# A hybrid decoder trunk on one core: seven places where the order of the engine programs changes

## The chip, the cores and the metric

The kernel runs on one core of a Trainium2 chip. The metric is the device time of one execution in microseconds (us); less is better. A core has a matrix engine (PE, with its weight loads as PEld), a vector engine (DVE), a scalar engine (ACT), a general engine (POOL, GpSimd) and a queue engine (SP) that here issues the loads. Each engine runs its own program in order; engines wait for one another on semaphores.

## The reference

Two layers. Each normalises x, multiplies it by one large matrix `w_in`, and feeds four token mixers from the product, 256 tokens long: a gated linear recurrence (LRU), a diagonal state space model (S5), retention, and native sparse attention (NSA, with compressed, selected and window keys). Cut to what matters here:

```python
def hybrid_layer(x, ...):
    proj = rms_norm(x, norm_g) @ w_in                 # 1024 -> 10008 columns
    u_lru, u_s5, qkv_ret, q_nsa, kv_nsa, bg_nsa, gate_paths, merge = split_columns(proj, IN_SIZES)
    ys = stack([lru(u_lru), s5(u_s5), retention(qkv_ret), nsa(q_nsa, kv_nsa, bg_nsa)])
    ys = ys * silu(gate_paths)
    branch = einsum('bsnw,nwd->bsnd', ys, w_branch)
    return x + sum(sigmoid(merge) * branch) @ w_out

def nsa(q, kv, bg):                                   # q: 8 heads of 64
    q = rope_half(q, pos, 500000, 16)                 # rotates the first 16 of 64 columns
    k_slc, k_win = rope_half(k_slc, ...), rope_half(k_win, ...)
    s = q @ k * 64 ** -0.5                            # softmax, times v, for each of the three paths
```

S5 needs powers of its complex step (from `exp`, `sin`, `cos` of the layer's parameters), an input matrix, an output matrix and a scan over blocks of four tokens. A final normalisation closes the stack.

## The kernel before, in words

**Tiling.** The large products are cut into chunks (`CHUNKS`, a table with an order written by hand): `u_s5`, `cmp`, `u_lru`, `ret_v`, `nsa_kv`, `ck`, `gate_s5`, `cv`, `gate_lru`, `merge_s5_0`, `merge_s5_1`, `ret_q`, `ret_k`, `nsa_q`, `glu_a`, `glu_b`, `gate_ret` and so on to `out_1b`. A chunk is made of weight units of 512 KB (128 x 1024 float32), numbered from 0; `UNIT_END[CHUNK[name]]` is the number of the unit behind a chunk. u_s5 has units 0 to 3, cmp 4 to 7, u_lru 8 to 11, ret_v 12 to 15, nsa_kv 16 to 19, gate_s5 20 to 23, gate_lru 24 to 27. Chunks write into two PSUM tensors in turn: `pr(name)` is `proj[CHUNK[name] % 2]`, and a chunk starts only when the chunk two before it has been evacuated (`evacuated[0]`, `evacuated[1]`; `evac`, `ev`).

**Three products for one.** Apart from the first three chunks, a unit is loaded by SP into one of four buffers `raw`, copied by ACT in a reduced float32 form as `w_hi` (`cast_units`, one of five slots), and the remainder `w_lo = raw - w_hi` is made by DVE (`split_lo` at L1247, for the chunks of `LO_ON_VECTOR`) or by POOL (`split_lo` at L676). PE multiplies w_hi by h_hi, w_hi by h_lo and w_lo by h_hi. A raw buffer is loaded again when its w_lo is done.

**Order.** Each engine has one program per layer (`@block.sync`, `gpsimd`, `scalar`, `vector`, `tensor`) written out by hand. What ACT does between casts is in small helpers: `next_cast(name)` casts units up to `UNIT_END + 4` and then waits for the chunk, `cast_units(n)` casts all units below n. All ACT operations have the line L698.

**S5 at a layer's start.** DVE makes input weights (`make_w`), ACT spreads them into `wbd` (`spread_w`), PE transposes them (`turn_w`), ACT copies the result (`keep_wT`) and turns the projected input into `uc` by sixteen small copies (`keep_u`). Then `state_inputs`, DVE's `scan_in`, `scan_steps`, `scan_out`, `state_outputs`, ACT's `keep_y`. `make_v` and `spread_v` do the output weights, `chunk_kernels` and `keep_ms` (sixteen copies) the kernel within a block, `angles` and `trig` the phases. All come twice, for half 0 and half 1. `parameters_a` and `parameters_b` work out the powers from the parameters; those of layer 1 run at the end of layer 0.

**The rest.** `compress` multiplies the blocks of keys and values by weights `ck` and `cv` that SP loads by four DMAs of 512 KB (`load_cw1`, at the units in `cw1_at`). `hidden` keeps the result, and a GELU follows (`hid_q`, `hid_tanh`). `rope_nsa` rotates sparse keys (`kd`) and query (`nq4`) in SBUF. `compressed_scores`, a softmax (`cs_sub`, `cs_exp`, `cp_ready`) and the transposes of `cmp_p` are the compressed path.

Of the kernel before, what the change touches and what calls it, by code (L numbers as in the profile page):

```python
# [90 lines left out]
def vector_splits(upto):  # L91
# [19 lines left out]
    "nT_done": 2, "nT_ready": 2, "noT_done": 1, "no_cmp": 1, "nrope_ready": 2, "out_token": 2, "qkT_done": 2,  # L111
    "qkT_ready": 2, "raw_loaded0": 448, "raw_loaded1": 448, "raw_loaded2": 448, "raw_loaded3": 448, "rnT_done": 1,
    "rn_ready": 1, "ro_done": 4, "rope_ready": 2, "rrstd": 1, "rs_done": 4, "rs_ready": 4, "rstd": 2, "rvar": 1,
    "sq": 4, "th_ready": 1, "th_sin": 3, "trig_done": 6, "u_ready": 1, "unit_used": 73, "v0_ready": 1,
    "v_ready": 2, "var": 2, "vbd_ready": 1, "vecT": 2, "vec_ready": 1, "vectors_loaded": 208, "vk_ready": 2,
    "vlo_done": 40, "wT_done": 4, "wT_ready": 4, "w_ready": 2, "wbd_ready": 2, "wl_loaded": 64, "xT_done": 4,
    "x_half": 3, "xc_ready": 1, "y_done": 2, "y_ready": 2, "yg_hi": 4, "yg_lo": 4, "yg_ready": 4, "yr_ready": 1,
    "z_arg": 1, "z_hi": 1, "z_lo": 1, "z_ready": 1, "z_tanh": 1}
# [1964 lines left out]
```

## Time and profile before

| | |
|---|---|
| median of 3 runs | 856.46 us (855.59 to 857.69) |
| the profiled execution | 856.7 us, its span 854.9 us |
| mean granted clock of PE over the span | 0.961 |
| PE busy | 796.3 us, 93% |
| DVE busy | 517.6 us, 61% |
| ACT busy | 450.9 us, 53% |
| POOL busy | 305.2 us, 36% |
| read from HBM | 124.85 MB, 147 GB/s |

The span goes from the first to the last instruction of the profiled execution. A granted clock of 1.00 is 2.4 GHz for PE, 0.50 is 1.2 GHz. Busy shares are means over stages of very different kinds: PE is busy for most of the span, and the other engines feed it. Layer 0 covers roughly the first 433 us, layer 1 the rest, with the same order of work.

### The profile page before, as it was taken

To read this page: it belongs to the slowest core of one execution; us is meant where nothing else is said; L and a number is where in the kernel's file an instruction comes from. 1 tells how busy PE (TensorE), PEld (TensorE's weight loads), DVE (VectorE), ACT (ScalarE), POOL (GpSimd) and SP (SyncE) were. 2 spreads that over 40 slices of the span, in tenths; PEclk is the share of its full clock that TensorE was granted. 3 is DMA by queue.
4 is the path that set the end of the run, shared out by engine and by line. 5 is a ranking of instruction groups with operands and counts; after the bars stand their busy time and mean duration, and the time that the engine had idled before them with its cause. 6 is when DMAs were issued, how large, how long until landed. Compare 5 with 4: busy or idle time off the path is not lost.

```text
span 854.9 us, 11525 instructions
## 1 busy us (share of the span) xinstructions
PE 796.3 (93%) x4446; PEld 680.7 (80%) x4446; DVE 517.6 (61%) x761; ACT 450.9 (53%) x781; POOL 305.2 (36%) x135
## 2 busy tenths in 40 slices
PE   8786999899989899999989979998998989999996
PEld 8675889688978688887878868986897868888885
DVE  2957394477698551534686575547868875435335
ACT  5555786345752356553447297654474534545542
POOL 3000000005468576657400000000256775655860
PEclk9977999999998799999999989999999998999999
DMA  8518355466245434345435663535635344345541
GB/s 250 140 50 289 99 176 178 138 191 193 88 117 169 134 118 153 102 150 171 145 78 140 196 216 94 204 123 165 211 121 156 114 137 127 126 129 170 173 148 49
DMA packets 86998, 126.64 MB, mean 148 GB/s; under 512 B 22072, under 2 KB 32672, under 8 KB 86944
## 3 DMA queue, kind: packets, MB, share of 16 engines
q1 hardware_dynamic: 86768, 125.88, 47.5%
q8 instruction: 35, 0.57, 0.3%
q14 instruction: 19, 0.16, 0.1%
q10 hardware_dynamic: 176, 0.04, 0.0%
HBM read 124.85 MB, written 1.05 MB: 147 GB/s over the span
## 4 chain that ended last, share of the span: by engine, by line
PE 73%; ACT 9%; DVE 8%; issue 5%; POOL 2%; DMA 2%; ACTq 0%; POOLq 0%; DVEq 0%
PE proj L1662 52%; PE proj L1701 5%; PE M L1657 3%; ACT sc L698 2%; DMA raw<-in_w_in 2%; POOL w_lo L676 2%; PE M L1823 2%; ACT nkT L698 1%; ACT qT L698 1%; PE M L1976 1%; PE M L1981 1%; DVE sc L1539 1%; PE M L559 1%; ACT w_hi L698 1%; PE M L1824 1%
## 5 line engine op out<-in xcount | busy, mean ns | idle before, releaser
L676 POOL TENSOR_TENSOR w_lo<-raw,w_hi 128x1024 fp32r<-128x1024 f32 x112 | 287.1, 2596 | 501.2 <-ACT w_hi L698 469.9
L698 ACT ACTIVATE w_hi<-raw 128x1024 fp32r<-128x1024 f32 x192 | 197.4, 1055 | 125.0 <-DMA raw<-in_w_in 68.1
L1662 PE MATMUL proj<-w_hi,h_hi 128*128 128x512 f32 x544 | 220.5, 405 | 8.2 <-DVE w_lo L1247 7.7
L1662 PE MATMUL proj<-w_lo,h_hi 128*128 128x512 f32 x544 | 215.6, 396 | 0.0
L1662 PE MATMUL proj<-w_hi,h_lo 128*128 128x512 f32 x544 | 215.2, 396 | 0.0
L1662 PEld LDWEIGHTS proj<-w_hi,h_hi 128*128 128x128 f32 x544 | 104.3, 192 | 31.7 <-DVE w_lo L1247 8.5
L1662 PEld LDWEIGHTS proj<-w_hi,h_lo 128*128 128x128 f32 x544 | 104.2, 192 | 22.8
L1662 PEld LDWEIGHTS proj<-w_lo,h_hi 128*128 128x128 f32 x544 | 104.4, 192 | 21.0 <-issue 0.5
L1247 DVE TENSOR_TENSOR w_lo<-raw,w_hi 128x1024 fp32r<-128x1024 f32 x80 | 94.8, 1221 | 38.5 <-ACT w_hi L698 27.1
L1701 PE MATMUL proj<-h_full,raw 128*128 128x256 f32 x256 | 59.3, 393 | 7.8 <-ACT u_s L698 7.8
L1701 PEld LDWEIGHTS proj<-h_full,raw 128*128 128x128 f32 x256 | 50.1, 198 | 15.5 <-ACT u_s L698 8.3
L698 ACT ACTIVATE sc<-sc,st 128x256 f32<-128x256 f32 x64 | 28.3, 448 | 57.2 <-DVE st L1555 57.2
L1662 PE MATMUL proj<-w_hi,ys_hi 128*128 128x512 f32 x128 | 52.7, 412 | 0.6 <-POOL w_lo L676 0.5
L1662 PE MATMUL proj<-w_lo,ys_hi 128*128 128x512 f32 x128 | 51.7, 404 | 0.0
L1662 PE MATMUL proj<-w_hi,ys_lo 128*128 128x512 f32 x128 | 51.4, 402 | 0.0
L698 ACT ACTIVATE qT<-M 32x128 f32<-32x128 f32 (+1 forms) x68 | 29.5, 433 | 35.2 <-PE M L1657 25.9
L1662 PE MATMUL proj<-h_hi,w_hi 128*128 128x256 f32 x128 | 36.9, 288 | 3.1 <-ACT nv L698 3.1
L1290 DVE SCALAR_TENSOR_TENSOR mt<-mt,proj 128x1024 f32<-128x1024 f32 x12 | 14.7, 1221 | 38.5 <-PE proj L1662 38.5
L1662 PE MATMUL proj<-h_lo,w_hi 128*128 128x256 f32 x128 | 36.2, 283 | 0.0
L1662 PE MATMUL proj<-h_hi,w_lo 128*128 128x256 f32 x128 | 36.2, 283 | 0.0
L1662 PEld LDWEIGHTS proj<-w_hi,ys_hi 128*128 128x128 f32 x128 | 25.2, 197 | 7.3 <-issue 1.3
L1662 PEld LDWEIGHTS proj<-w_hi,ys_lo 128*128 128x128 f32 x128 | 25.1, 196 | 5.5
(330 smaller groups left out, 1294.0 us busy)
## 6 DMA issues: line engine op xcount, KB each, us to landing
raw<-in_w_in SPq DMA_DIRECT2D x152, 512.0 KB, 3.7
raw<-in_w_branch SPq DMA_DIRECT2D x32, 512.0 KB, 3.6
raw<-in_w_out SPq DMA_DIRECT2D x16, 512.0 KB, 3.6
raw<-in_s_w_glu SPq DMA_DIRECT2D x8, 512.0 KB, 4.5
raw<-in_w_in SPq DMA_DIRECT2D x8, 256.0 KB, 2.6
merged<-in_nsa_ck_w SPq DMA_DIRECT2D x4, 512.0 KB, 5.2
mt<-in_nsa_ck_w SPq DMA_DIRECT2D x4, 512.0 KB, 6.8
merged<-in_nsa_cv_w SPq DMA_DIRECT2D x4, 512.0 KB, 4.6
```

What stands on the lines that cost most here:

```text
L559: last = nc.tensor.matmul(M[:, k // 2, at:at + P], x[:, t, k * P:(k + 1) * P], diag[:, t, :], start=True, stop=True)
L676: nc.gpsimd.tensor_tensor(w_lo[:, slot(s, l), 0:n * w], raw[:, u % N_RAW, 0:n * w], w_hi[:, slot(s, l), 0:n * w].bitcast(f32), ALU.subtrac ...
L698: i = nc.scalar.activation(out_, in_, func, **kw)
L1247: v.tensor_tensor(w_lo[:, slot(s, l), 0:w], raw[:, u % N_RAW, 0:w], w_hi[:, slot(s, l), 0:w].bitcast(f32), ALU.subtract).then_inc(vlo_done, 1)
L1290: v.scalar_tensor_tensor(m, m, 1.0, src, ALU.add, ALU.mult).then_inc(evac(full), 1)
L1539: i = v.tensor_tensor(cp[:, e_], cmp_s[:, e_], bc(coef[:, e_].unsqueeze(3), shape), ALU.mult)
L1657: return nc.tensor.transpose(dst, src, ident[0:rows_, 0:rows_])
L1662: last = mm(dst, left[i], right[j], start=start and n == 0, stop=stop and n == 2, skip_group_check=True)
L1701: last = mm(ps[:, m * T:(m + 1) * T], rw[:, m * P:(m + 1) * P], h_full[:, k, :], start=st_ and m % 2 == 0, stop=sp_, skip_group_check=True)
L1823: mm(dst, vk[:, f, s, 1:LC + 1].rearrange("p k g c -> p (k g c)"), s5_h[:, f, s, :], start=f == 0, stop=False)
L1824: last = mm(dst, ms[:, s, :], uc[:, HS * h + s, :], start=False, stop=True)
L1976: last_ = mm(M[:, 2, at:at + P], nqT[r, 2 * h + n, 0:P], nkT[r, i, 0:P], start=True, stop=True)
```

## The change

- `u_s5` is evacuated on ACT right behind its chunk, ahead of `spread_w(0)`; `keep_v0` goes ahead of `trig(0)`; `keep_u` reads the SBUF copy.
- `spread_v(0)` goes behind the copies of `cmp`; `u_lru` is evacuated behind three casts fewer; `spread_w(1)` goes ahead of the casts of units 15 and 16, `keep_ms(0)` behind them; the four `ck` loads go from ahead of unit 15 to ahead of unit 17.
- The copies of `nsa_kv` no longer stand behind two casts.
- `hid_tanh` goes ahead of `merge_chunk("s5", 0)`.
- The exponential of the compressed scores goes ahead of the `qT` copy.
- The rotation of the keys moves to behind `skip(1)`; that of the query to behind `rope_ret(1, "ret_k")`, reading PSUM, with the factor 64 ** -0.5 in new constants; `chunk("glu_b")` on PE waits for its reads.
- The second part of `parameters_b` becomes `parameters_c` and runs at the start of the next layer's DVE program.

The table of semaphore counts and the removed helper are left out of the diff.

```diff
@@ sync
-                    cw1_at = {UNIT_END[CHUNK["u_lru"]] + 3: "ck", UNIT_END[CHUNK["gate_s5"]] + 2: "cv"}
+                    cw1_at = {UNIT_END[CHUNK["ret_v"]] + 1: "ck", UNIT_END[CHUNK["gate_s5"]] + 2: "cv"}
@@ scalar
-                        src = pr("u_s5")[:, :].rearrange("p (q c j) -> p q c j", q=KB, j=LC)[:, :, :, LC - 1 - e]
+                        src = u_s5[:, :, :].rearrange("p q (c j) -> p q c j", j=LC)[:, :, :, LC - 1 - e]
...
+                    next_cast("u_s5")
+                    run(flat(u_s5[:, :, :]), pr("u_s5")[:, :], ACT.Copy, evac("u_s5"))
                     spread_w(0)
+                    keep_v0()
                     trig(0)
-                    keep_v0()
-                    next_cast("u_s5")
+                    act.wait_ge(evac("u_s5"), ev("u_s5"))
                     keep_u(0)
                     keep_u(1)
                     keep_wT(0, 0)
                     keep_u(2)
                     keep_u(3)
-                    run(flat(u_s5[:, :, :]), pr("u_s5")[:, :], ACT.Copy, evac("u_s5"))
                     keep_wT(0, 1)
-                    spread_v(0)
...
                     run(bgate[:, :, :], cm[:, :, 256:CMP_W], ACT.Tanh, cmp_read, scale=0.5)
+                    spread_v(0)
...
-                    next_cast("u_lru")
+                    cast_units(UNIT_END[CHUNK["u_lru"]] + 2)
+                    act.wait_ge(chunk_done, ch("u_lru"))
                     run(u_lru[:, :, 3:T + 3], pr("u_lru")[:, :].rearrange("p (t n) -> p t n", t=KB), ACT.Copy, evac("u_lru"))
+                    cast_units(UNIT_END[CHUNK["u_lru"]] + 3)
+                    spread_w(1)
+                    cast_units(UNIT_END[CHUNK["ret_v"]])
+                    keep_wT(1, 0)
                     cast_units(UNIT_END[CHUNK["ret_v"]] + 1)
-                    spread_w(1)
                     keep_ms(0)
-                    keep_wT(1, 0)
                     next_cast("ret_v")
...
-                    next_cast("nsa_kv")
+                    act.wait_ge(chunk_done, ch("nsa_kv"))
...
-                    merge_chunk("s5", 0)
                     act.wait_ge(hid_arg, 1)
                     run(hid_q, hid_q, ACT.Tanh, hid_tanh, scale=GELU_C)
+                    merge_chunk("s5", 0)
...
+                    act.wait_ge(cs_sub, 1)
+                    run(cols(3072, 256), cols(3072, 256), ACT.Exp, cs_exp)
                     act.wait_ge(rnT_done, 1)
                     run(flat(qT[:, :, :]), MF[:, 1024:2048], ACT.Copy, yr_ready)
-                    act.wait_ge(cs_sub, 1)
-                    run(cols(3072, 256), cols(3072, 256), ACT.Exp, cs_exp)
@@ vector
                         link(v.tensor_tensor(S(17), S(19), S(16), ALU.subtract))
+
+                    def parameters_c(s):
+
+                        stage = Layer(vector, s)
                         stage.wait_ge(th_sin, 3)
...
+                    parameters_c(l)
                     v.memset(u_lru[:, :, 0:3], 0.0)
...
+                    nk4 = kd[:, :, :, :, :, :].rearrange("p a y h u d -> p a (y h u) d")
+
+                    def rotate(src, dst, at, read):
+
+                        shape = [P, TT, NHQ, 8]
+                        cos, sin = (bc(cst(f"nsa_{f}{at}").rearrange("p (a c) -> p a c", a=TT).unsqueeze(2), shape) for f in ("cos", "sin"))
+                        x1, x2_ = src[:, :, :, 0:8], src[:, :, :, 8:16]
+                        v.tensor_tensor(rope_n[:, 0], x1, cos, ALU.mult)
+                        v.tensor_tensor(rope_n[:, 1], x2_, sin, ALU.mult)
+                        v.tensor_tensor(rope_n[:, 2], x2_, cos, ALU.mult)
+                        v.tensor_tensor(rope_n[:, 3], x1, sin, ALU.mult).then_inc(read, 1)
+                        dve.wait_ge(read, 1)
+                        v.tensor_tensor(dst[:, :, :, 0:8], rope_n[:, 0], rope_n[:, 1], ALU.subtract)
+                        v.tensor_tensor(dst[:, :, :, 8:16], rope_n[:, 2], rope_n[:, 3], ALU.add).then_inc(nrope_ready, 1)
...
                     skip(1)
+                    rotate(nk4, nk4, "", nk_read)
                     split_lo("merge_s5_0", 0)
...
-                    dve.wait_ge(evac("nsa_kv"), ev("nsa_kv"))
-                    dve.wait_ge(rope_ready, 2)
-                    rope_nsa(rope_nsa_kd)
-
+                    dve.wait_ge(evac("nsa_q"), ev("nsa_q"))
                     dve.wait_ge(nrope_ready, 1)
+                    rotate(pr("nsa_q")[:, :].rearrange("p (a h c) -> p a h c", a=TT, h=NHQ), nq4, "_q", nq_read)
+
+                    dve.wait_ge(nrope_ready, 2)
...
-                    dve.wait_ge(evac("nsa_q"), ev("nsa_q"))
-                    dve.wait_ge(yg_ready, 1)
-                    rope_nsa(nq4)
                     gate_times("ret")
@@ tensor
+                    pe.wait_ge(nq_read, 1)
                     chunk("glu_b")
```

## Rows read from the trace of the kernel before

**Rows 1.** Waits of PE: who waited for whom, us in total, times, longest.
```profile
PE M L1657 <- ACT gate L698: 13.0, 2, 7.1
PE M L1657 <- DVE sc L1539: 8.5, 2, 4.2
PE proj L1701 <- ACT u_s L698: 7.8, 2, 7.2
PE proj L1662 <- DVE w_lo L1247: 7.7, 2, 3.8
PE M L559 <- DVE diag L552: 4.6, 2, 3.7
PE M L1657 <- DVE u_s L1433: 4.1, 2, 2.0
PE proj L1662 <- ACT nv L698: 3.1, 2, 1.6
```

**Rows 2.** Windows: length, busy PE, PEld, DVE, ACT, POOL, granted clock, DMA share.
```profile
45.70:51.50 5.80, 5.76 (x14) 4.54 (x15) 4.04 (x19) 4.39 (x9) 0.00 (x0) 0.50 0.01 3
80.30:85.60 5.30, 5.25 (x17) 4.48 (x18) 5.20 (x8) 5.08 (x17) 0.00 (x0) 0.50 0.66 169
163.50:167.50 4.00, 4.00 (x11) 3.13 (x12) 3.30 (x3) 0.59 (x1) 0.00 (x0) 0.58 0.65 212
273.40:280.20 6.80, 6.80 (x21) 5.50 (x21) 1.33 (x4) 0.00 (x0) 1.99 (x1) 0.50 0.47 153
290.60:297.20 6.60, 6.57 (x23) 5.44 (x24) 1.93 (x3) 1.33 (x2) 4.51 (x2) 0.50 0.73 213
...
497.80:502.00 4.20, 4.20 (x14) 3.72 (x15) 4.17 (x5) 4.04 (x15) 0.00 (x0) 0.50 0.69 165
...
662.50:665.90 3.40, 3.40 (x10) 2.63 (x9) 2.11 (x5) 3.35 (x4) 0.00 (x0) 0.50 0.22 85
705.40:713.70 8.30, 8.30 (x27) 6.79 (x28) 3.63 (x4) 1.37 (x3) 4.43 (x2) 0.50 0.69 210
```

**Rows 3.** Timeline of ACT in layer 0: start us, us, what, [idle before].
```profile
28.31 0.42 ACT L698 ACTIVATE gate<-qT 64x256 f32<-64x256 f32 x1 [7.66 <-DVE sc L1154]
...
41.55 3.08 ACT L698 ACTIVATE nkT<-proj 32x256 f32<-32x256 f32 x8
...
110.62 2.01 ACT L698 ACTIVATE w_hi<-raw 128x1024 fp32r<-128x1024 f32 x2
...
114.26 4.92 ACT L698 ACTIVATE s5x<-M 32x64 f32<-32x64 f32 x16
```

**Rows 4.** Chain of waits in layer 1: start us, us, what.
```profile
485.16 7.13 DMA raw<-in_w_in
...
506.39 0.87 PE M L1657 x8
507.26 5.47 PE proj L1662 x24
```

**Rows 5.** Timeline of DVE in layer 0.
```profile
68.14 1.23 DVE L1247 TENSOR_TENSOR w_lo<-raw,w_hi 128x1024 fp32r<-128x1024 f32 x1 [1.12 <-ACT w_hi L698]
...
71.74 1.20 DVE L1205 TENSOR_TENSOR_SCAN sc<-sc 128x512 f32<-128x512 f32 x1
...
77.16 0.68 DVE L1217 TENSOR_TENSOR s5x<-sc 128x504 f32<-128x504 f32 x1
...
87.40 3.50 DVE L1247 TENSOR_TENSOR w_lo<-raw,w_hi 128x1024 fp32r<-128x1024 f32 x3 [0.23 <-ACT w_hi L698]
```

**Rows 6.** Timeline of DVE at hid's tanh, layer 0.
```profile
158.19 0.23 DVE L1375 TENSOR_SCALAR kT<-kT 128x128 f32<-128x128 f32 x1 [8.93 <-ACT kT L698]
```

**Rows 7.** Timeline of DVE behind the exponential, layer 0.
```profile
282.33 0.50 DVE L1529 TENSOR_TENSOR sc<-sc,const 128x128 f32<-128x128 f32 x2 [6.49 <-ACT sc L698]
```

**Rows 8.** DVE's groups, 200 to 246 us: busy us, mean ns, idle before.
```profile
L1428 DVE TENSOR_TENSOR sc<-u_s,const 128x128 f32<-128x128 f32 x1 | 2.5, 2475 | 0.0
```

**Rows 9.** Timeline of DVE at the layers' border.
```profile
435.81 0.68 DVE L1635 SCALAR_TENSOR_TENSOR x<-proj,x 128x512 f32<-128x512 f32 x1
```

More of the change, by code:

```diff
@@ L110 @@
     "mT_done": 2, "mag_arg": 1, "mag_exp": 1, "mhi_done": 2, "mlo_done": 2, "ms_ready": 2, "mt_free": 6,
[L111 to L118, printed above, removed]
+    "nT_done": 2, "nT_ready": 2, "nk_read": 1, "noT_done": 1, "no_cmp": 1, "nq_read": 1, "nrope_ready": 2,
+    "out_token": 2, "qkT_done": 2, "qkT_ready": 2, "raw_loaded0": 448, "raw_loaded1": 448, "raw_loaded2": 448,
+    "raw_loaded3": 448, "rnT_done": 1, "rn_ready": 1, "ro_done": 4, "rope_ready": 2, "rrstd": 1, "rs_done": 4,
+    "rs_ready": 4, "rstd": 2, "rvar": 1, "sq": 4, "th_ready": 1, "th_sin": 3, "trig_done": 6, "u_ready": 1,
+    "unit_used": 73, "v0_ready": 1, "v_ready": 2, "var": 2, "vbd_ready": 1, "vecT": 2, "vec_ready": 1,
+    "vectors_loaded": 208, "vk_ready": 2, "vlo_done": 40, "wT_done": 4, "wT_ready": 4, "w_ready": 2,
+    "wbd_ready": 2, "wl_loaded": 64, "xT_done": 4, "x_half": 3, "xc_ready": 1, "y_done": 2, "y_ready": 2,
+    "yg_hi": 4, "yg_lo": 4, "yg_ready": 4, "yr_ready": 1, "z_arg": 1, "z_hi": 1, "z_lo": 1, "z_ready": 1,
+    "z_tanh": 1}
 TWO_PI = 2.0 * math.pi
@@ L131 @@
 for _n, _s in (("ident", P), ("ret_cos", TT * 64), ("ret_sin", TT * 64), ("nsa_cos", TT * 8), ("nsa_sin", TT * 8),
+               ("nsa_cos_q", TT * 8), ("nsa_sin_q", TT * 8),
                ("cmp_cos", 8), ("cmp_sin", 8), ("decay", NH_RET * T), ("causal", 2 * P), ("cmp_add", TT * 16),
@@ L160, in shape_constants @@
     put("nsa_cos", c), put("nsa_sin", s)
+    put("nsa_cos_q", c * f32(HD ** -0.5)), put("nsa_sin_q", s * f32(HD ** -0.5))
     c, s = rope((np.arange(32) % 16) * 16 + 31, 500000.0, HD // 4)
@@ L360, in hybrid_trunk @@
             "at_even", "at_s", "at_max", "at_exp", "at_pT", "at_pT_ready", "at_o", "at_no"))
-        noT_done = sem("noT_done")
+        noT_done, nk_read, nq_read = sem("noT_done"), sem("nk_read"), sem("nq_read")
         mT_done, mhi_done, mlo_done = sem("mT_done"), sem("mhi_done"), sem("mlo_done")
@@ L1420, in _ @@
                     rope_ret(1, "ret_k")
-                    def rope_nsa(x4):
-                        shape = [P, TT, NHQ, 8]
-                        cos = bc(cst("nsa_cos").rearrange("p (a c) -> p a c", a=TT).unsqueeze(2), shape)
-                        sin = bc(cst("nsa_sin").rearrange("p (a c) -> p a c", a=TT).unsqueeze(2), shape)
-                        x1, x2_ = x4[:, :, :, 0:8], x4[:, :, :, 8:16]
-                        v.tensor_tensor(rope_n[:, 0], x1, cos, ALU.mult)
-                        v.tensor_tensor(rope_n[:, 1], x2_, sin, ALU.mult)
-                        v.tensor_tensor(rope_n[:, 2], x2_, cos, ALU.mult)
-                        link(v.tensor_tensor(rope_n[:, 3], x1, sin, ALU.mult))
-                        v.tensor_tensor(x1, rope_n[:, 0], rope_n[:, 1], ALU.subtract)
-                        v.tensor_tensor(x2_, rope_n[:, 2], rope_n[:, 3], ALU.add).then_inc(nrope_ready, 1)
-                    rope_nsa_kd = kd[:, :, :, :, :, :].rearrange("p a y h u d -> p a (y h u) d")
-                    dve.wait_ge(evac("nsa_kv"), ev("nsa_kv"))
-                    dve.wait_ge(rope_ready, 2)
-                    rope_nsa(rope_nsa_kd)
+                    dve.wait_ge(evac("nsa_q"), ev("nsa_q"))
                     dve.wait_ge(nrope_ready, 1)
+                    rotate(pr("nsa_q")[:, :].rearrange("p (a h c) -> p a h c", a=TT, h=NHQ), nq4, "_q", nq_read)
+                    dve.wait_ge(nrope_ready, 2)
                     dve.wait_ge(chunk_done, ch("glu_a"))
```

## The prediction

> **What bounds the kernel now.** I read the waits of PE first, then the granted clock by stretch, then the timelines of ACT and DVE around each wait. PE stands still for 51.7 us of the 854.9 us span (the sum of its idle stretches); for the rest it works, so only what ends a PE wait, or what makes a matmul quicker, can move the end. [rows 1] shows that nearly all of it has a few releasers, each met once a layer: ACT's spread of the S5 weights (13.0), DVE's product for the compressed attention (8.5), ACT's copy of the S5 input (7.8), a DVE remainder w_lo (7.7), the diagonal at a layer's end (4.6, of which 3.7 at the border of the layers), the rotated sparse query (4.1) and ACT's copy of the sparse keys and values (3.1). The second view is the windows of [rows 2]: after most of these waits the granted clock is 0.50, the 1.2 GHz level, for 3.4 to 8.3 us in which PE works. There are ten such stretches; the four short ones are shown by their first and last. Their PE busy times are 5.8, 5.3, 6.8, 6.6, 4.2, 8.3 and four of about 3.4, together 50.5 us. At half clock half of that is lost: 25.3 us. The waits and the low clock together are 77 us, the most that an order of the queues could give.
>
> **Seven edits, part by part.** The sum is made against the profiled execution: span 854.9 us, time 856.7 us (0.24 above the median of 856.46).
>
> 1. *u_s5 evacuated first.* proj[0] comes free for u_lru only when ACT has copied u_s5; before, that copy stood behind sixteen small copies (keep_u), two wT copies, trig(0) and spread_w(0). Now it follows the chunk at once, and keep_u reads the copy in SBUF. In layer 0 PE's 7.2 goes, in layer 1 its 0.7: the 7.8 of [rows 1]. What is late next: state_inputs(0), which wants keep_u and both wT copies. In layer 1 ACT now blocks on the chunk before it does spread_w(0) and trig(0). After the chunk it has 15.8 us of work (copy 1.0, spread_w 2.5, keep_v0 1.6, trig 2.6, twice 3.1 of keep_u, twice 1.0 of wT), while PE has some 17.2 (turn_c, cmp, two turn_w, half of u_lru). 1.3 us of cover, so the cost is nothing; without cover each us is a us.
> The keep_u copies change their source. In [rows 3] eight 256-column copies from PSUM took 3.08, 0.385 each, and one from SBUF 0.42: sixteen cost 0.6 more, and 0.7 of cover stays. The Trainium skill (VectorE: DVE Perf Modes, "The TRN2 errata") speaks against this edit here: it has ScalarE pay 52 cycles more per instruction from SBUF than from PSUM. By its figure sixteen copies are 0.7 us more, an estimate; the trace agrees, and the sum would be the same by either.
>
> 2. *ck loads two units later, spread_w(1) ahead of the fourth cast.* Before, turn_w(1, 0) waited 7.1 and 6.0: ACT sat on the cast of unit 15 before spread_w(1), and that unit landed 7.1 us after its issue [rows 4] because four 512 KB loads of the compression weights stood ahead of it on SP. Now SP sends units 15 and 16 first and spread_w(1) needs only chunk_kernels(0). The 13.0 of [rows 1] goes. The ck weights come some 3 us later and are wanted only at compress, more than 25 us on, so that move costs nothing; SP's wait on v_ready and vk_ready holds unit 17 only, by then both are there.
> What is late next is DVE. Let T be the end of chunk_kernels(0). ACT has unit 14's w_hi at T+1.0 (u_lru is done at T-1.1, copy, cast). From the start of that w_lo, DVE takes 4.8 to the end of scan_steps (68.14 to 72.94), then w_lo 15 1.2, then 10.0 from the first line of scan_out to the end of angles(1) (77.16 to 87.17), then w_lo 17 1.2 [rows 5]: unit 17 is ready at T+18.2. PE wants it after two half chunks of 5.7, two transposes of 1.0 and a unit of 2.75 ([rows 4], 5.5 and 0.9 without overlap): T+16.2. A **new wait of about 2.1 us** in each layer, 4.2. Bounds: 0 if DVE's small gaps close, 4 each if keep_ms(0), which now stands ahead of cast 17, meets a late load.
>
> 3. *Two casts taken from ahead of the kv copies.* nv is ready 2.0 sooner, so the 3.1 of [rows 1] goes. But casts 22 and 23 now follow keep_ms(1). With N the end of nsa_kv: kv copies to N+1.9, keep_ms 4.9, casts 2.0 [rows 3], the hidden copy 0.4: N+9.2; PE has kernels 1.1, compress 1.9 and six us of gate_s5 and wants it at N+8.8. w_lo 22 is at N+9.0, scan_out 3.8 behind it, w_lo 23 at N+13.9, wanted at N+12.6. **New waits of 0.4 and 1.3**, less overlap 1.6 a layer, 3.2 in all: this edit gives nothing. Bounds 2 and 5.
>
> 4. *hid's tanh ahead of merge_chunk(s5, 0).* DVE stood 8.9 for it [rows 6] and then still had three operations of the GELU before the w_lo that PE waited for. ACT passes that place some ten us sooner, DVE has the argument by then, so the cast units behind it wait for nothing. DVE has ten us of slack: the 7.7 goes.
>
> 5. *Exponential ahead of the qT copy.* DVE stood 6.5 for it [rows 7], and its next three operations on two SBUF inputs each lasted as long as a POOL w_lo. Its argument is ready at 275.8, the copy ahead of it at 282.0. The 8.5 goes, with some five us to spare; next late is yr_ready, over before PE gets there. For that the qT copy is 0.4 later at most.
>
> 6. *Sparse rotations.* The key rotation moves to a DVE gap of 2.0 after skip(1), where POOL has no w_lo; six operations at the 0.25 of [rows 7] are 1.5, covered. The query rotation reads PSUM straight after ret_k's. In its old place each of four operations lasted 2.5 [rows 8]. The 4.1 of [rows 1] goes and DVE has 15 us less in a layer. Added: glu_b waits for nq_read. DVE gets the copy at 208.1, four operations, read by 209.5, wanted at 216.9: covered by lru_mm and glu_a. The last two have both inputs in SBUF and may last 2.5 each; glu_a's evacuation, queued behind them, is due at 216.4, so still nothing.
>
> 7. *parameters_c behind the layer's border.* The last half of x was added at 435.81 [rows 9], though PE had been done since 433.3 (its 3.7 wait before 437.0). 2.5 goes, 1.2 stays. Its 4.3 us now lie ahead of layer 1's S5 preparation: w_ready at about 445.6, wanted by ACT only after the u_s5 chunk, at 453.
>
> **Sum.** Waits: 7.8 + 13.0 + 3.1 + 7.7 + 8.5 + 4.1 = 44.2, plus 2.5 = 46.7, less 4.2 and 3.2: 39.3. Clock: 25.3 now. In two places the trace is split: the 273.4 stretch has no long idle ahead of it, only the compressed scores' tiny matmuls, and layer 1 had none there; and a 2.05 wait was followed by a low stretch in layer 1 (662.5) but not in layer 0. So I keep 3.4 for the first and 1.7 for one of the two new 2.1 waits, 5.1 in all; 20.2 comes back. 39.3 + 20.2 = 59.5, and 856.7 - 59.5 = 797.2; I say **797**.
>
> **Rivals.**
> - *The feeding side takes over in the first third* (17 in 100): ACT's and DVE's queues are fuller than my two chains show, and the waits at units 17 and 23 grow to 4 and 2.5 each with low clock behind them. Against my 7.4: 13.0, and some 5 of clock; 807, and 812 with half of edit 4 lost. For it: DVE is busy in almost all of that stretch. Against it: both layers have the same queues and the chain adds up from rows.
> - *The clock does not come back* (10 in 100): the low stretches belong to the kind of work, not to the waits. All 20.2 stay: 817. For it the 273.4 stretch; against it, eight of the ten stand right behind a wait.
> - *No new wait* (8 in 100): my two chains are too long by a few us each and the clock is full. 797.2 - 7.4 - 5.1 = 784.7.
> - *An edit does not bite* (3 in 100): one copy or load is released by something else than the trace names, of the size of edit 2: 13.0 + 4.7 of clock, 814.
> - *Slower* (2 in 100): one mechanism, PE's clock over dense stretches. With the waits gone PE works almost without rest, and if a dense stretch itself brought 1.2 GHz, each 10 us of it would cost 5. The gain is gone from about 120 us of it on top, over the kernel; now there are 50.5, none of them in a dense stretch. From there it is slower, 860 for 126 us.
>
> **How the numbers follow.** Forecast 60 in 100, its own range 790 to 804. With 784.7 on one side and 807 to 817 on the other, 784 to 816 leaves out under 2 in 10. The measurement tells 0.3% (2.6 us) from nothing; only the last rival and a mishap I don't see lie there: faster 0.95, same 0.02, slower 0.03.
>
> **What would show it.** After: no PE wait on u_s or gate of over 1 us; on w_lo of DVE four waits of 1 to 2.5, at unit 17 of nsa_kv and unit 23 of gate_s5; mean clock from 0.961 to about 0.99; DVE's rotations about 0.3 each and POOL's w_lo a little shorter. Wrong if state_inputs(0) of layer 1 waits for u_ready (edit 1's cover was too small), if cast 17 waits on a DMA, or if low-clock stretches stand where no wait is.

## The result, and the profile after

The changed kernel takes **816.65 us** (median of 4 runs, 812.21 to 819.84), the kernel before 856.03 on the same chip: a ratio of 0.9537, 95% interval 0.9475 to 0.9598. That is 39.4 us less, where 59.5 were forecast, and the time lies 0.65 above the forecast's range. The profiled execution took 819.8 us. From the page of the changed kernel, its span, the busy time of PE and PE's granted clock in 40 slices:

```profile
span 818.0 us, 11525 instructions
PE 788.7 (96%) x4446; PEld 677.6 (83%) x4446; DVE 479.4 (59%) x761; ACT 459.3 (56%) x781; POOL 304.3 (37%) x135
...
PEclk9979899999999999999999899999999989999999
```

Two subtractions divide the result. Span less PE busy went from 58.6 to 29.3: 29.3 us less standing still, against 39.3 forecast. PE busy went from 796.3 to 788.7: 7.6 us back from the clock, against 20.2. So of the profiled run's 22.6 us above the forecast, 10.0 are waits and 12.6 are matmuls that ran at the lower level. ACT, with the same 781 instructions, is 8.4 us busier than the 450.9 of before; that is the trace of the cause, as the copies below show.

The waits of PE after, where [rows 1] had those of before (waiter, releaser, us in total, times, longest; L1673 is the old L1662, L1807 is `state_inputs`, L701 is ACT's one line):

```profile
PE M L1807 <- ACT s5x L701: 7.6, 2, 4.2
PE proj L1673 <- DVE w_lo L1259: 7.6, 4, 2.6
PE proj L1673 <- POOL w_lo L679: 2.0, 4, 0.8
PE M L562 <- DVE diag L555: 1.9, 2, 1.1
PE proj L1750 <- ACT kT L701: 1.5, 2, 0.8
```

Every wait that the edits aimed at is gone: gate, the product `sc`, `u_s` of ACT and of DVE, `nv`. The first line is new and was forecast as nothing: `state_inputs(0)` waits once a layer for `keep_wT`. The second has nearly the sum that it had in [rows 1] (7.7) by chance: it is now unit 17 (2.63 and 2.60) and unit 23 (1.20 twice), which were forecast at 2.1 and 1.3.

The chain that ended last shows the first line's making. Layer 1, from the end of the u_s5 chunk (start us, us, what):

```profile
424.96 6.92 PE proj L1712 x32
...
432.83 1.23 ACT gate L701 x3
434.06 0.01 issue
434.07 1.23 ACT gate L701 x3
...
438.08 1.34 ACT sc L701 x3
439.42 0.57 ACT nkT L701
439.99 0.01 issue
440.00 0.68 ACT nkT L701
...
451.24 1.03 ACT s5x L701
452.27 0.14 issue
452.41 5.42 PE M L1807 x32
```

The chain leaves PE at 431.88 and comes back to it at 452.41. In between ACT hardly rests: copy of u_s5, `spread_w(0)`, `keep_v0`, `trig(0)`, sixteen `keep_u` (nkT) and two `keep_wT`. That is 20.4 us to 452.27; PE had work until 448.95. The length of the sixteen, from the timeline of ACT (start us, us, what):

```profile
439.32 5.48 ACT L701 ACTIVATE nkT<-u_s 32x256 f32<-32x256 f32 x8
444.81 1.02 ACT L701 ACTIVATE s5x<-M 128x1024 f32<-128x1024 f32 x1
445.86 5.36 ACT L701 ACTIVATE nkT<-u_s 32x256 f32<-32x256 f32 x8
```

Eight copies take 5.48 and 5.36, 0.67 to 0.68 each, where [rows 3] has eight from PSUM in 3.08. Same shape, same type, same count; only the source is another.

The windows of low clock, where [rows 2] had ten (length, busy PE, PEld, DVE, ACT, POOL, granted clock, DMA share, GB/s). There are six, besides one at the very end:

```profile
10.50:13.90 3.40, 3.40 (x17) 3.40 (x17) 0.25 (x4) 0.00 (x0) 0.00 (x0) 0.50 1.00 396
51.50:61.70 10.20, 10.20 (x41) 9.48 (x41) 2.99 (x6) 6.36 (x12) 0.00 (x0) 0.50 0.00 0
85.60:92.40 6.80, 6.20 (x17) 5.03 (x18) 4.04 (x4) 5.80 (x9) 0.00 (x0) 0.50 0.71 231
263.10:266.50 3.40, 3.40 (x9) 2.66 (x10) 2.75 (x9) 0.42 (x1) 1.40 (x1) 0.50 0.48 164
454.20:461.00 6.80, 6.80 (x28) 6.30 (x28) 1.85 (x4) 4.86 (x10) 0.00 (x0) 0.50 0.02 4
659.00:665.80 6.80, 6.80 (x22) 5.70 (x22) 3.60 (x13) 0.42 (x1) 2.46 (x1) 0.50 0.54 157
```

PE works 36.8 us in them at 0.50, the 1.2 GHz level, and loses half, 18.4. The second and the fifth begin 0.6 and 1.8 us behind the new wait (PE works again from 50.86 and 452.41) and cost 8.5 of the 18.4. The first stands at the first transposes of layer 0; the profile of before has none there, and four of the twelve kernels below have one, so no single edit brings it. The third stands at unit 17's wait of layer 0, and layer 1, with the same wait, has none. The fourth and the sixth stand at the compressed scores with no wait ahead of them.

Four more answers to rows of before, in the timeline of DVE: the first GELU operation behind hid's tanh [rows 6], the product behind the exponential [rows 7], the last of the six operations of the query's rotation [rows 8], and the last half of x at the border [rows 9].

```profile
146.54 0.22 DVE L1403 TENSOR_SCALAR kT<-kT 128x128 f32<-128x128 f32 x1
...
265.26 0.49 DVE L1540 TENSOR_TENSOR sc<-sc,const 128x128 f32<-128x128 f32 x2 [0.48 <-ACT sc L701]
...
200.70 2.47 DVE L1319 TENSOR_TENSOR u_s<-sc 128x128 f32<-128x128 f32 x1
...
413.21 0.69 DVE L1646 SCALAR_TENSOR_TENSOR x<-proj,x 128x512 f32<-128x512 f32 x1 [0.94 <-PE proj L1673]
```

In the edited places DVE's waits on ACT of 8.93 and 6.49 are gone or 0.48, and x is added right behind PE.

### The profile page after: what moved, and what is told of

Read it like the earlier page. It is cut to its first block, busy times and chain, and to the rows that moved or that the text cites. A ratio compares the mean times of both kernels' runs of the same rounds, so it can differ in the third digit from the quotient of the medians.

```text
span 818.0 us, 11525 instructions
## 1 busy us (share of the span) xinstructions
PE 788.7 (96%) x4446; PEld 677.6 (83%) x4446; DVE 479.4 (59%) x761; ACT 459.3 (56%) x781; POOL 304.3 (37%) x135
## 4 chain that ended last, share of the span: by engine, by line
PE 72%; issue 9%; DVE 8%; ACT 7%; POOL 4%; DMA 1%; POOLq 0%; DVEq 0%; SPq 0%; ACTq 0%
PE proj L1673 52%; POOL w_lo L679 4%; PE proj L1712 3%; ACT nkT L701 3%; PE M L1668 2%; PE M L1807 2%; DVE w_lo L1259 2%; PE M L1834 2%; ACT sc L701 1%; PE M L1988 1%; PE M L562 1%; PE M L1993 1%; PE M L1958 1%; PE M L1835 1%; PE M L2012 1%
## 5 line engine op out<-in xcount | busy, mean ns | idle before, releaser
L701 ACT ACTIVATE w_hi<-raw 128x1024 fp32r<-128x1024 f32 x192 | 197.2, 1053 | 95.9 <-PE proj L1673 60.0
L1673 PE MATMUL proj<-w_hi,h_hi 128*128 128x512 f32 x544 | 219.3, 403 | 6.7 <-DVE w_lo L1259 5.2
L1673 PE MATMUL proj<-w_lo,h_hi 128*128 128x512 f32 x544 | 214.7, 395 | 0.0
L1673 PE MATMUL proj<-w_hi,h_lo 128*128 128x512 f32 x544 | 214.5, 394 | 0.0
L1673 PEld LDWEIGHTS proj<-w_hi,h_hi 128*128 128x128 f32 x544 | 103.6, 190 | 30.1 <-DVE w_lo L1259 6.1
L1673 PEld LDWEIGHTS proj<-w_hi,h_lo 128*128 128x128 f32 x544 | 103.7, 191 | 22.4
L1673 PEld LDWEIGHTS proj<-w_lo,h_hi 128*128 128x128 f32 x544 | 103.8, 191 | 20.7 <-issue 0.5
L701 ACT ACTIVATE sc<-sc,st 128x256 f32<-128x256 f32 x64 | 28.2, 442 | 49.4 <-DVE st L1566 49.4
L1673 PE MATMUL proj<-w_hi,ys_hi 128*128 128x512 f32 x128 | 50.9, 397 | 0.5 <-POOL w_lo L679 0.5
L1673 PE MATMUL proj<-w_lo,ys_hi 128*128 128x512 f32 x128 | 49.9, 390 | 0.0
L1673 PE MATMUL proj<-w_hi,ys_lo 128*128 128x512 f32 x128 | 49.9, 390 | 0.0
L701 ACT ACTIVATE qT<-M 32x128 f32<-32x128 f32 (+1 forms) x68 | 29.5, 434 | 19.1 <-PE M L1668 12.5
L1673 PE MATMUL proj<-h_hi,w_hi 128*128 128x256 f32 x128 | 37.1, 290 | 2.4 <-DVE w_lo L1259 2.4
L1673 PE MATMUL proj<-h_lo,w_hi 128*128 128x256 f32 x128 | 36.2, 283 | 0.0
L1673 PE MATMUL proj<-h_hi,w_lo 128*128 128x256 f32 x128 | 36.2, 283 | 0.0
L701 ACT ACTIVATE s5x<-M 32x64 f32<-32x64 f32 (+4 forms) x72 | 27.0, 375 | 5.0 <-PE M L1668 4.2
L1673 PEld LDWEIGHTS proj<-w_hi,ys_hi 128*128 128x128 f32 x128 | 24.0, 188 | 6.0 <-issue 0.8
```

The source lines that it names most:

```text
L701: i = nc.scalar.activation(out_, in_, func, **kw)
L1673: last = mm(dst, left[i], right[j], start=start and n == 0, stop=stop and n == 2, skip_group_check=True)
```

## Experiments

Theory A: the reads of `keep_u` are the fault. It takes every fourth value of u_s5 (`(c j)` with a fixed j), which from PSUM cost 0.385 and from SBUF 0.68; the new wait and the clock behind it follow. Rival B: the chain on ACT is too long anyhow with the chunk in its middle. Rival C: the clock stays low for reasons other than waits. The recorded expectations letter their own theories anew, run by run. Then each edit was undone alone, to see which term of the sum is of the wrong size.

| kernel | median us | span, profiled | PE busy | span less PE busy |
|---|---|---|---|---|
| before | 856.03 | 854.9 | 796.3 | 58.6 |
| changed | 816.65 | 818.0 | 788.7 | 29.3 |
| adjacent reads | 799.09 | 800.7 | 778.7 | 22.0 |
| trig(0) later | 802.35 | 799.6 | 773.8 | 25.8 |
| both of these | 798.63 | 796.7 | 774.5 | 22.2 |
| edit 1 undone | 805.68 | 803.0 | 772.1 | 30.9 |
| edit 2 undone | 832.37 | 831.9 | 791.8 | 40.1 |
| edit 3 undone | 817.31 | 815.8 | 786.7 | 29.1 |
| edit 4 undone | 829.27 | 827.4 | 790.2 | 37.2 |
| edit 5 undone | 827.58 | 824.4 | 786.1 | 38.3 |
| edit 6 undone | 821.3 | 819.1 | 785.3 | 33.8 |
| edit 7 undone | 817.22 | 822.0 | 790.2 | 31.8 |
| scores in two halves | 800.1 | 798.6 | 775.8 | 22.8 |
| three repairs | 794.13 | 791.5 | 775.3 | 16.2 |

Each median is of 4 runs. The kernel before was timed again beside each group of runs, with medians of 855.57 to 856.76; the changed kernel was timed once, so every difference below shares its 816.65 and its scatter. A time that goes up and down from run to run does so with the clock: the changed kernel's four were 819.78, 813.52, 812.21 and 819.84 us at mean granted clocks of 0.976, 0.984, 0.986 and 0.976. One per cent of clock is some 8 us, so the last two columns, from one execution each, must be read beside the median. The waits repeat from profile to profile (the 7.6 on DVE's w_lo stands in seven of these kernels); the clock does not.

### Adjacent reads for keep_u

```diff
-  src = u_s5[:, :, :].rearrange("p q (c j) -> p q c j", j=LC)[:, :, :, LC - 1 - e]
+  src = u_s5[:, :, :].rearrange("p q (j c) -> p q j c", j=LC)[:, :, LC - 1 - e, :]
...
-  run(flat(u_s5[:, :, :]), pr("u_s5")[:, :], ACT.Copy, evac("u_s5"))
+  run(u_s5[:, :, :].rearrange("p q (j c) -> p q j c", j=LC),
+      pr("u_s5")[:, :].rearrange("p (q c j) -> p q j c", q=KB, j=LC), ACT.Copy, evac("u_s5"))
```

The copy of the chunk turns the order, so that `keep_u` reads runs of 64 adjacent values; DVE's one reader of u_s5 follows.

> The changed kernel with one edit: the copy of u_s5 is written with each token's place in its block outermost, so that keep_u reads 64 contiguous values per row instead of every fourth; skip reads u_s5 through the same view. Theory A (the stride): from SBUF every fourth value is what made keep_u 0.68 us each instead of 0.385; contiguous they go to 0.42, ACT is 4.2 us earlier a layer, the waits of 4.2 and 3.4 at state_inputs(0) go to under 0.6 and the low-clock stretch behind each (10.2 and 6.8 us) goes with them: 816.7 - 7.0 - 8.5 = about 801. Theory B (the source, not the stride): any copy of 256 columns from SBUF to 32 partitions costs 0.68, the waits and the time stay within 2 us of 816.7.

Measured: 799.09 us (797.51 to 802.48), ratio 0.9334 (0.9302 to 0.9367). The timeline of ACT in layer 1 and the last line of the waits of PE:

```profile
428.99 3.39 ACT L701 ACTIVATE nkT<-u_s 32x256 f32<-32x256 f32 x8
...
PE M L1809 <- ACT s5x L701: 0.2, 1, 0.2
```

Eight copies in 3.39, 0.42 each: the very figure that the prediction took from one small copy in [rows 3]. The wait of 7.6 is 0.2, and the time is 2 us from the forecast 797.2. In the profiled runs 7.3 us of standing still and 10.0 of PE busy have gone. A holds, and the theory of the recorded text that any copy from SBUF costs 0.68 whatever its stride falls. B falls too: the order of ACT's queue is the same and the wait is gone. C falls for most of the loss: PE busy is 17.6 under that of before, though the work is the same; four low stretches are left. Here is the same stretch of PE's timeline in layer 1, of the changed kernel and then of this one:

```profile
452.41 5.42 PE L1807 MATMUL M<-nkT,s5x 128*128 128x64 f32 x32 [3.46 <-ACT s5x L701]
```

```profile
438.45 3.68 PE L1809 MATMUL M<-nkT,s5x 128*128 128x64 f32 x32
```

The wait has gone, and the products behind it are 1.7 us quicker.

### trig(0) behind the weights

The reads stay every fourth value; only 2.5 us of other work leave the chain, `trig(0)` going behind `keep_wT(0, 1)`.

```diff
                     keep_v0()
-                    trig(0)
...
                     keep_wT(0, 1)
+                    trig(0)
```

> The changed kernel with trig(0) moved behind keep_wT(0, 1) on ACT; keep_u still reads every fourth value from SBUF. Theory A (ACT's queue between the u_s5 copy and keep_wT(0, 1) sets state_inputs(0)): the waits fall by trig's 2.6 us, from 4.2 and 3.4 to 1.6 and 0.8, and the low clock behind them shrinks or goes: 816.7 - 5.2 - 0 to 8 = 803 to 811. Theory B (something else releases state_inputs, such as u_lru's loads): same time, the waits stay.

Measured: 802.35 us (801.4 to 810.4), ratio 0.9398 (0.9341 to 0.9455). Waits of PE:

```profile
PE proj L1673 <- DVE w_lo L1259: 8.6, 4, 3.1
PE M L1807 <- ACT s5x L701: 2.2, 2, 1.1
```

Shortening the chain by 2.5 took 5.4 of the 7.6 away, and unit 17's waits grew by 0.5 each. So the wait is one of the chain's length, as A and B both have it, and its price is far more than its length: 14.3 us of median for 4.4 us of waits. The rest is clock: two stretches of 3.4 us in this profile instead of six with 37.4. The time lies just under the 803 to 811 expected.

### Both repairs

> Two repairs of edit 1 at once: the copies of kept u read adjacent values, and trig(0) stands behind the weights of the keep. Either alone takes the wait ahead of state_inputs(0) away or to about 1 us (799.09 and 802.35). If that wait is the whole cost of edit 1's miss, the two together give what adjacent reads alone give, 798 to 800. If the length of the copies on ScalarE costs something elsewhere too, or trig(0) does where it stands, the two differ: below 796 would show the second, above 802 the lateness of trig(0) at unit 17.

Measured: 798.63 us (798.52 to 798.74), ratio 0.9329 (0.9315 to 0.9343). Not to be told from adjacent reads alone, as expected if the wait is the whole cost of edit 1's miss. Once ACT is within PE's 17.1 us, more room there is worth nothing that these runs show.

### Each edit undone

*Edit 1*: `keep_u` reads PSUM again (that line is left out here) and u_s5 is evacuated behind it.

```diff
-                    next_cast("u_s5")
-                    run(flat(u_s5[:, :, :]), pr("u_s5")[:, :], ACT.Copy, evac("u_s5"))
                     spread_w(0)
-                    keep_v0()
                     trig(0)
+                    keep_v0()
+                    next_cast("u_s5")
...
                     keep_u(3)
+                    run(flat(u_s5[:, :, :]), pr("u_s5")[:, :], ACT.Copy, evac("u_s5"))
```

> The changed kernel with edit 1 undone: u_s5 copied last, keep_u from PSUM, trig and spread_w as before. By my ledger edit 1 took out a wait of 7.2 and 0.7 and put in 4.2 and 3.4, so it is worth about nothing in waits: the time is 817 give or take 3, with a wait of 7 us on u_s in layer 0 and under 1 in layer 1. By the prediction's step it was worth 7.8 us plus 2.9 of clock: 827.

Measured: 805.68 us (804.64 to 813.1), ratio 0.9424 (0.9376 to 0.9473): faster with the edit undone, by 11.0 in the medians, though one of its four runs (813.1) lies above the changed kernel's lowest (812.21). Neither number expected. In PE's timeline of layer 0 and the one window of low clock of this kernel:

```profile
45.92 8.82 PE L1711 MATMUL proj<-h_full,raw 128*128 128x256 f32 x32 [7.13 <-ACT u_s L701]
...
42.50:49.30 6.80, 3.38 (x8) 2.75 (x9) 6.49 (x19) 6.69 (x16) 0.00 (x0) 0.50 0.01 2
```

The waits are as long as with the edit (30.9 against 29.3 of standing still): the edit exchanged 7.8 of old waits and 0.6 of a small one for 7.6 of new ones. The difference is PE busy, 772.1 against 788.7, 16.6 less in two profiled executions that lie 15.0 apart. Against the kernel with adjacent reads, undoing the edit costs 6.6 us (805.68 to 799.09): with the right reads edit 1 does pay, for the 7.8 of waits that it removes. Half of the low window here falls into the wait itself, where it costs nothing; in the changed kernel PE worked through all 17.0 us of the two behind `state_inputs`. Its four other stretches (two of them at the compressed scores) aren't in this profile either, and no row says why. One of the four runs, at 813.1 and a clock of 0.982 instead of 0.994, had some, by its clock.

*Edit 2*: `ck` loads, casts, `spread_w(1)`, `spread_v(0)` and the u_lru copy as before.

```diff
-  cw1_at = {UNIT_END[CHUNK["ret_v"]] + 1: "ck", ...
+  cw1_at = {UNIT_END[CHUNK["u_lru"]] + 3: "ck", ...
...
-                    cast_units(UNIT_END[CHUNK["u_lru"]] + 3)
-                    spread_w(1)
-                    cast_units(UNIT_END[CHUNK["ret_v"]])
-                    keep_wT(1, 0)
                     cast_units(UNIT_END[CHUNK["ret_v"]] + 1)
+                    spread_w(1)
                     keep_ms(0)
+                    keep_wT(1, 0)
```

> The changed kernel with edit 2 undone: ck loads ahead of unit 15, spread_w(1) behind the cast of unit 15, spread_v(0) and the u_lru copy in their old places. By the prediction's ledger: the waits of 7.1 and 6.0 at turn_w(1, 0) come back with 4.7 of clock, and the two of 2.6 at unit 17 of nsa_kv go: 816.7 + 13.1 - 5.2 + 1 to 5 = 826 to 830. Rival, that with edit 1 in its slow form ACT's delay at state_inputs(0) is passed on and the load is early enough: under 820.

Measured: 832.37 us (825.8 to 833.7), ratio 0.9714 (0.9673 to 0.9754): the edit is worth 15.7. Waits of PE:

```profile
PE M L1665 <- ACT gate L701: 15.0, 2, 8.4
...
PE proj L1670 <- DVE w_lo L1256: 2.4, 2, 1.2
```

15.0 come back and unit 17's 5.2 go, 9.8 net (13.0 less 4.2 forecast, 8.8). The time is above the 826 to 830 expected. In the profiled pair, 13.9 apart, standing still is 10.8 and PE busy 3.1 longer; this profile has seven low stretches with some 54 us, in part inside waits, instead of six with 37.4.

*Edit 3*: the two casts ahead of the nsa_kv copies again.

```diff
-                    act.wait_ge(chunk_done, ch("nsa_kv"))
+                    next_cast("nsa_kv")
```

> The changed kernel with edit 3 undone: casts 22 and 23 ahead of the nsa_kv copies. The prediction had it worth nothing: waits of 1.6 a layer on nv come back, and those at hidden_T and unit 23 of gate_s5 (0.8 and 1.2) go: within 1.5 us of 816.7. Rival, that it was worth its full 3.1: 820.

Measured: 817.31 us (816.7 to 819.41), ratio 0.9546 (0.9518 to 0.9573). Waits of PE:

```profile
PE proj L1673 <- DVE w_lo L1259: 5.2, 2, 2.6
PE proj L1673 <- ACT nv L701: 3.1, 2, 1.6
```

3.1 back on nv; the kT line (1.5) and unit 23 (2.4) gone. It is the exchange that the prediction worked out, and the time doesn't move.

*Edits 4 and 5*: `merge_chunk("s5", 0)` ahead of hid's tanh again, and the `qT` copy ahead of the exponential again.

The recorded expectation of edit 4 names two exponential and copy steps, which are edit 5's; the edit that was run, and the 7.7 us that it is about, are edit 4's.

```diff
+                    merge_chunk("s5", 0)
                     run(hid_q, hid_q, ACT.Tanh, hid_tanh, scale=GELU_C)
-                    merge_chunk("s5", 0)
```

> Edit 4 alone is undone: order of the two exponential and copy steps as before. Prediction's step: it removed 7.7 us of waits. If it holds, these waits come back and nothing else moves: 816.65 + 7.7 = 824, and up to 828 if a stretch of low clock (3.4 us each, as the changed kernel's rows have them) follows each of the waits. Rival: what was gained there is taken back by the next wait, so undoing it costs under 3 us, 817 to 820.

```diff
-                    act.wait_ge(cs_sub, 1)
-                    run(cols(3072, 256), cols(3072, 256), ACT.Exp, cs_exp)
                     act.wait_ge(rnT_done, 1)
                     run(flat(qT[:, :, :]), MF[:, 1024:2048], ACT.Copy, yr_ready)
+                    act.wait_ge(cs_sub, 1)
+                    run(cols(3072, 256), cols(3072, 256), ACT.Exp, cs_exp)
```

> The changed kernel with edit 5 undone: the exponential behind the qT copy. By the ledger a wait on DVE's L1539 line of up to 4.2 a layer comes back with 3 to 4 of low clock each; but DVE's three operations there may now meet another state of POOL. 816.7 + 8.5 + 7.5 = 833 if all of it; rival, that POOL's contention was a matter of timing and the wait is shorter now: 820 to 826.

Measured: 829.27 us (828.83 to 829.36), ratio 0.9686 (0.967 to 0.9702), and 827.58 (823.78 to 829.01), ratio 0.9666 (0.9638 to 0.9694). Edit 4 is worth 12.6 (829.27 is above the 824 to 828 expected), edit 5 10.9 (827.58 lies between the 833 of the full price and the rival's 820 to 826). From the waits and the windows of the first, then of the second:

```profile
PE proj L1673 <- DVE w_lo L1259: 15.3, 6, 3.8
...
156.50:163.20 6.70, 5.08 (x12) 4.02 (x13) 4.97 (x5) 1.49 (x2) 0.00 (x0) 0.50 0.55 182
559.30:566.00 6.70, 5.90 (x14) 4.65 (x15) 4.55 (x5) 2.29 (x3) 0.00 (x0) 0.50 0.68 208
```

```profile
PE M L1668 <- DVE sc L1550: 8.4, 2, 4.2
...
272.20:279.00 6.80, 5.37 (x20) 4.53 (x21) 2.14 (x2) 1.33 (x2) 5.91 (x3) 0.50 0.78 229
675.00:681.70 6.70, 5.72 (x21) 4.79 (x22) 2.04 (x2) 1.33 (x2) 5.45 (x3) 0.50 0.79 233
```

The waits come back at their old length (15.3 less 7.6 is 7.7; 8.4), all four with a low stretch that reaches on behind them, some 11 us of work at half speed in either kernel, 5.5 lost. 7.7 + 5.5 is 13.2 for 12.6 measured; 8.4 + 5.5 is 13.9 for 10.9. That sum is not shown as the cause of the medians: PE busy of the whole profile is only 1.5 above the changed kernel's with edit 4 undone and 2.6 below it with edit 5 undone, because other stretches were shorter or missing (behind the wait at `state_inputs` of layer 0, 6.8 us instead of 10.2 with edit 5 undone).

*Edit 6*: both rotations in their old places, in SBUF.

```diff
-                    rotate(nk4, nk4, "", nk_read)
...
-                    rotate(pr("nsa_q")[:, :].rearrange(...), nq4, "_q", nq_read)
+                    rotate(nk4, nk4, "", nk_read)
...
+                    rotate(nq4, nq4, "", nq_read)
...
-                    pe.wait_ge(nq_read, 1)
```

> Edit 6 alone is undone. Prediction's step: 4.1 us of waits. If it holds, 816.65 + 4.1 = 821, up to 824 with one stretch of low clock more per layer (1.7 us each). Rival: hidden by what is late next, 816 to 818.

*Edit 7*: `parameters_c` of layer 1 at the end of layer 0 again.

```diff
-                    parameters_c(l)
+                    if l == 0:
+                        parameters_c(0)
...
+                        parameters_c(l + 1)
```

> Edit 7 alone is undone. Prediction's step: 2.5 us of waits. If it holds, 816.65 + 2.5 = 819, up to 822 with a stretch of low clock. Rival: hidden by what is late next, 816 to 818.

Measured: 821.3 us (820.92 to 824.13), ratio 0.9601 (0.9583 to 0.9619), and 817.22 (816.1 to 823.82), ratio 0.9562 (0.9523 to 0.9602). The line that came back in each, from the waits of PE:

```profile
PE M L1670 <- DVE u_s L1319: 4.1, 2, 2.0
```

```profile
PE M L562 <- DVE diag L555: 4.5, 2, 3.7
```

4.1 and 2.6 of waits, as forecast. Edit 6 is worth 4.7 by the medians; all four of its runs lie above all four of the changed kernel's, the nearest two by 1.1. For edit 7 the medians show 0.6, which the runs (816.1 to 823.82) can't tell from the 2.5 of its wait nor from nothing.

The seven together: -11.0 + 15.7 + 0.7 + 12.6 + 10.9 + 4.7 + 0.6 = 34.2, against 39.4. The 5.2 between are no more than the scatter by the clock, and the seven differences share one median: were it 1 us off, the sum would be 7 off.

### The compressed scores in two halves

On top of adjacent reads, the second half of the 32 tiny products is moved one call on, to see whether they are what lowers the clock there.

```diff
                     compressed_scores(0)
-                    compressed_scores(1)
...
+                    compressed_scores(1)
```

> The kernel contig (799.1) with the second half of the compressed scores moved behind the next weight unit on PE, so that its 32 tiny products come as 16 and 16. Theory A (the low clock of 3.4 and 6.8 us there belongs to the stretch of tiny products): it goes, 1.7 + 3.4 less, 794 to 796, and runs scatter less. Theory B (it follows from something else): the stretches stay, 799 give or take 1.5.

Measured: 800.1 us (799.25 to 800.44), ratio 0.935 (0.9336 to 0.9364). The windows around both places and the low ones of this profile:

```profile
76.70:80.10 3.40, 3.40 (x9) 2.63 (x8) 1.22 (x2) 3.37 (x7) 0.00 (x0) 0.50 0.88 267
250.00:257.00 7.00, 7.00 (x43) 5.94 (x43) 2.16 (x7) 0.82 (x2) 2.71 (x1) 1.00 0.45 157
465.80:472.60 6.80, 6.16 (x17) 5.05 (x18) 4.08 (x4) 5.03 (x8) 0.00 (x0) 0.50 0.71 221
640.00:649.00 9.00, 9.00 (x59) 7.91 (x60) 4.20 (x7) 0.86 (x2) 4.71 (x2) 1.00 0.49 175
```

The clock stays at the 2.4 GHz level at the scores now, but one profile in which it does is no proof (those of edit 1 undone and of trig(0) later have no stretch there either, with the products together). The stretch at unit 17 came in layer 1 as well, 6.8 us where adjacent reads alone had none, and the time is that of adjacent reads alone: the stretches go as theory A has it, the time is theory B's. Whether the tiny products lower the clock stays open.

### Three repairs in one kernel

Adjacent reads, and the two new waits that the prediction had named: unit 17's w_lo ahead of DVE's `angles(1)`, and casts 22 and 23 ahead of `keep_ms(1)` but still behind the nsa_kv copies.

```diff
+                    cast_units(UNIT_END[CHUNK["nsa_kv"]] + 4)
...
+                    split_lo("nsa_kv", 1)
...
-                    split_lo("nsa_kv", 1, 2, 3)
+                    split_lo("nsa_kv", 2, 3)
```

> The kernel contig (799.1) with two more moves: split_lo of unit 17 of nsa_kv ahead of angles(1) on DVE, and casts 22 and 23 ahead of keep_ms(1) on ACT. If the waits of 2.6 at unit 17 (twice) stand behind angles(1) alone and those of 1.2 at unit 23 (twice) behind keep_ms(1), both go down to 0.3 or less: 799.1 - 4.8 - 2.2 = 792, and 790 with the low clock behind the first. Rival, that ACT's keep_ms(0), still ahead of cast 17, or a late load holds unit 17: 796 to 799.

Measured: **794.13 us** (788.5 to 795.9), ratio 0.927 (0.9227 to 0.9313), the fastest here. Waits of PE:

```profile
PE proj L1754 <- ACT kT L701: 2.4, 2, 1.2
PE proj L1677 <- POOL w_lo L679: 2.0, 4, 0.7
...
PE proj L1677 <- ACT nv L701: 1.0, 2, 0.5
```

No wait on DVE's w_lo is left: 7.6 go, 0.9 come on kT and 1.0 on nv. Standing still falls from 22.0 to 16.2, 5.8, for 5.0 of median. Because of the 1.9 that came back elsewhere, the time lies between the 790 to 792 expected and the rival's 796 to 799. All lines of its waits together are 9.2 us, the most that ending waits could still give; the clock is on top, three stretches of 3.4 us in this profile, and the run of 788.5 had a mean granted clock of 0.998 where the profiled one, 793.37, had 0.992.

## Why the prediction was wrong, step by step

**Edit 1 failed: its "so the cost is nothing".** `state_inputs(0)` was to wait for nothing and waited 7.6 us. Two things were wrong in that step. First the price of the source. The prediction took 0.42 for a copy from SBUF, from a row whose source lies in runs of adjacent values, and put it to a copy that takes every fourth float; that was 0.68. It made sixteen copies cost 0.6 us more where they cost 4.7 (10.84 against 6.16). The rest of that chain was right: 15.8 and 4.7 make 20.5, where 20.4 were measured, and PE's cover was 17.1 for 17.2. So 1.3 of cover became waits of 3.4 in layer 1 and 4.2 in layer 0, the case that the last lines of the prediction name as the one to make it wrong. Second, layer 0's chain wasn't added up at all; there DVE's phases hold ACT up for 0.8 more. The row for the right price was missing from the trace of before, and then both ends should have stood: 0.42 and something well above it. At 0.68 the step would have said 3.4 us of wait a layer, and with 1.7 to 4.2 of clock behind each (the stretches of 3.4 to 8.3 us in [rows 2]) 807 to 812. The measured median is 4 above that still: the rest is the clock, below.

The Trainium skill has the rule (Advanced Engine Details and Errata, "SBUF Cachelines"): SBUF is read in lines of 16 bytes, and a reader that goes to another line with each access pays for it. Every fourth float32 lies 16 bytes from the last, and the trace agrees with the direction: 0.68 us against 0.42 for 256 values. The prediction weighed another place of the Trainium skill (VectorE: DVE Perf Modes, "The TRN2 errata"), by which ScalarE pays 52 cycles more per instruction from SBUF than from PSUM. Adjacent reads bear it out (3.39 for eight against 3.08); the reads as written cost far more.

**The clock term was mis-sized.** Forecast 20.2 back of 25.3; the changed kernel's profile gives 7.6 of busy time. That profile is near the changed kernel's slow end, 3.1 above its median. 10.0 of the 12.6 missing came back with adjacent reads, so they hung on the wait at `state_inputs` or went with it. The remainder is what the prediction treated too firmly: which waits have a stretch behind them. Unit 17's wait of 2.6 had one in layer 0 of the changed kernel (6.8) and none in layer 1; with the scores in two halves it was longer in layer 1; the compressed scores, which it took as one stretch of 3.4, had 3.4 and 6.8. From run to run the changed kernel moves by 7.6 us in this way. The 5.1 kept for what stays should have been a range: the four kernels with the new wait repaired and the wait at unit 17 left kept some 3 to 8.4 (half of the work in the low stretches). Why a wait has a stretch behind it in one layer or run and not in another, no run here shows.

**What held.** Unit 17: 2.1 forecast, 2.6 measured; unit 23: 1.3 and 1.2; hidden's copy 0.4 and 0.8; the border 1.2 left and 1.1. Edits 4, 5, 6 and 7 took away the waits that they were said to, to 0.1 us by the lines that undoing them brings back; edit 2's came back at 15.0 for 13.0. The medians move the same way for edits 2, 4, 5 and 6: 15.7, 12.6, 10.9 and 4.7. Edit 3 gave nothing, as worked out. With adjacent reads both terms of the sum come out close: the forecast makes 19.3 of standing still and 776.1 of PE busy, the profile has 22.0 and 778.7, in the slowest of its four runs. Two of the rotation's operations were allowed 2.5 each; one took it (2.47), the other five 0.3, and none mattered. Not foreseen: PE waits 2.0 on POOL's w_lo, 1.0 before.

**The rivals.** The measured time is that of "the clock does not come back" (817), but that is chance: its reason, that the work itself holds the clock down, does not hold. With the same kind of work, five kernels above had PE busy of 772 to 776. (The prediction counts eight of the ten low stretches of before behind a wait; by the trace it is nine, all but that of 273.4.) "The feeding side takes over" named units 17 and 23 with 4 and 2.5; they had 2.6 and 1.2. What happened was in no rival: the feeding side, at another place.

## What to carry to other kernels

When a change gives an instruction another source, its price is that of the new memory at the same stride, so look for a row with both, and where there is none, keep both ends. Add up the whole queue between a chunk's end and the next product that needs it, in every layer, also where an old wait is about to go. What a wait costs is its length plus the half-speed work behind it, and the second part depends on where the stretch falls, which no row of before foretold: give it as a range, and judge a change by several runs.
